# Last layer's mixer: gate projections in half blocks with two weight areas, a third convolution lane, gate columns taken together

## The reference

```
def _state_features(h, w_in_l, conv_l, a_log_l, dt_bias_l):
    p = h @ w_in_l[:, :N_STATE]
    ...
    gkv = jax.nn.silu(_dwconv(p[..., 2 * RET_W:2 * RET_W + 2 * GDN_W], conv_l[:, GDN_W:])).astype(jnp.float32)
    gk = _l2norm(_split_heads(gkv[..., :GDN_W], H_GDN))
    ...
    log_a = -jnp.exp(a_log_l.astype(jnp.float32))[:, None, :, None] * jax.nn.softplus(
        gab[0] + dt_bias_l.astype(jnp.float32)[:, None, :, None])
    beta = jax.nn.sigmoid(gab[1])
def _query_features(h, w_in_l, conv_l):
    ...
    gq = jax.nn.silu(_dwconv(p[..., 2 * RET_W:2 * RET_W + GDN_W], conv_l[:, :GDN_W])).astype(jnp.float32)
    gq = _l2norm(_split_heads(gq, H_GDN)) * GDN_DK ** -0.5
    gz = p[..., 2 * RET_W + GDN_W:2 * RET_W + 2 * GDN_W]
    gates = jax.nn.sigmoid(p[..., 2 * RET_W + 2 * GDN_W:].astype(jnp.float32))
def _mixer_out(ret_o, gdn_o, rg, gz, gates, ret_gn_w_l, gdn_norm_w_l, w_ret_out_l, w_gdn_out_l, w_o_l):
    ret_y = _merge_heads(_group_norm(ret_o)) * ret_gn_w_l.astype(jnp.float32) * jax.nn.silu(rg.astype(jnp.float32))
    gdn_y = _merge_heads(_head_rms(gdn_o)) * gdn_norm_w_l.astype(jnp.float32) * jax.nn.silu(gz.astype(jnp.float32))
    merged = (gates[..., :D_MODEL] * (ret_y.astype(dt) @ w_ret_out_l)
              + gates[..., D_MODEL:] * (gdn_y.astype(dt) @ w_gdn_out_l))
    return merged.astype(dt) @ w_o_l
```

## Time and profile before

| | us |
|---|---|
| median of 3 runs | 3236.97 (3236.73 to 3237.56) |
| profiled execution, its own time | 3248.51 |
| its span in the trace | 3246.7 |

### The profile page before, as it was taken

How to read it: one execution, slowest core, us unless ns; L and a number is a source line. 1 busy time by engine, 2 the same in 40 slices (tenths; PEclk the granted TensorE clock), 3 DMA queues, 4 the chain that set the end, 5 groups by cost and what they waited for, 6 DMA issues and landing times.

```text
span 3246.7 us, 29030 instructions
## 1 busy us (share of the span) xinstructions
PE 2499.2 (77%) x9500; PEld 1318.0 (41%) x9500; DVE 1623.4 (50%) x3307; ACT 835.9 (26%) x2259; POOL 831.3 (26%) x717
## 2 busy tenths in 40 slices
PE   6788897877979877888877777778787767576673
PEld 3665343423545455733322222456554433222221
DVE  4535645769876663565667654355524332111112
ACT  1212334243433230233343433223110101011110
POOL 1002332344546110133444433011010012222221
PEclk9689998998989977999999999888988779788886
DMA  6027997897979812499999999410112189999992
GB/s 254 1 78 288 368 366 293 324 396 272 371 296 371 338 52 78 168 405 414 416 421 395 421 422 421 164 65 26 52 52 109 76 338 397 393 386 384 383 375 84
DMA packets 128898, 885.92 MB, mean 273 GB/s; under 512 B 23008, under 2 KB 23392, under 8 KB 31584
## 3 DMA queue, kind: packets, MB, share of 16 engines
q0 software_dynamic: 86976, 553.74, 43.3%
q1 hardware_dynamic: 41760, 330.22, 25.4%
HBM read 877.56 MB, written 37.75 MB: 282 GB/s over the span
## 4 chain that ended last, share of the span: by engine, by line
PE 44%; DMA 24%; DVE 20%; ACT 5%; issue 4%; POOL 2%; SPq 1%; DVEq 0%; POOLq 0%; ACTq 0%
PE ps L155 43%; DMA ring<-in_peer_uv,idx_u 10%; DMA ring<-in_w_gu 5%; DVE ring L1256 5%; DVE arena L76 4%; ACT arena L125 3%; DMA ring<-in_w_down 3%; DMA arena<-in_w_gu 2%; DVE arena L97 1%; PE ps L158 1%; DVE ring L76 1%; DVE iu L113 1%; SPq L2479 1%; DVE arena L1256 1%; DMA ring<-in_w_in 1%
## 5 line engine op out<-in xcount | busy, mean ns | idle before, releaser
L155 PE MATMUL ps<-ring,arena 128*128 128x512 f32 (+3 forms) x3200 | 1239.6, 649 | 305.4 <-ACT arena L125 183.6
L155 PEld LDWEIGHTS ps<-ring,arena 128*128 128x128 f32 (+2 forms) x3200 | 459.5, 180 | 984.4 <-issue 593.9
L1256 DVE CUSTOM_DVE_ANT_0 ring<-ring,h 128x1024 f32<-128x1024 f32 x428 | 539.6, 1261 | 392.0 <-DMA ring<-in_peer_uv,idx_u 365.1
L155 PE MATMUL ps<-arena 128*128 128x128 f32 (+7 forms) x2184 | 514.4, 425 | 201.4 <-ACT arena L125 83.6
L2297 POOL DMA_INDIRECT ring<-in_peer_uv,idx_u x428 | 464.5, 1085 | 798.5 <-PE ps L155 667.0
L125 ACT ACTIVATE arena<-arena 128x1 f32<-128x1 f32 (+4 forms) x1121 | 309.6, 276 | 818.0 <-DVE arena L1256 731.9
L155 PEld LDWEIGHTS ps<-arena 128*128 128x128 f32 (+3 forms) x2184 | 296.6, 202 | 382.2 <-issue 153.9
L155 PE MATMUL ps<-ring,hT 128*128 128x512 f32 (+1 forms) x704 | 327.1, 621 | 44.2 <-DMA ring<-in_w_in 22.1
L76 DVE TENSOR_TENSOR arena<-arena,ps 128x512 f32<-128x512 f32 (+1 forms) x134 | 77.2, 576 | 449.0 <-ACT arena L125 353.3
L125 ACT ACTIVATE arena<-ps 128x512 f32<-128x512 f32 (+5 forms) x164 | 89.7, 547 | 762.5 <-PE ps L155 692.3
L125 ACT ACTIVATE arena<-cst,arena 128x128 f32<-128x128 f32 x512 | 206.3, 403 | 199.3 <-PE ps L155 159.8
(11 more groups left out here) (116 smaller groups left out, 1621.7 us busy)
## 6 DMA issues: line engine op xcount, KB each, us to landing
ring<-in_w_gu SPq DMA_DIRECT2D x98, 1024.0 KB, 30.3
ring<-in_w_down SPq DMA_DIRECT2D x52, 1024.0 KB, 22.6
ring<-in_w_in SPq DMA_DIRECT2D x22, 2048.0 KB, 9.1
arena<-in_w_gu SPq DMA_DIRECT2D x30, 1024.0 KB
ring<-in_w_mod SPq DMA_DIRECT2D x12, 2048.0 KB, 11.1
ring<-in_peer_wq SPq DMA_DIRECT2D x8, 2048.0 KB, 7.8
ring<-in_w_o SPq DMA_DIRECT2D x6, 2048.0 KB, 11.6
arena<-in_w_down SPq DMA_DIRECT2D x12, 1024.0 KB
```

What stands on the lines that cost most here:

```text
L155: return self.e.matmul(o, lhsT, rhs, start=start, stop=stop, skip_group_check=True)
L1256: v.done(v.e.tensor_tensor_reduce(out=row, in0=row, in1=h[:, n // 128, :], scale=1.0, scalar=0.0, op0=ALU.mult, op1=ALU.add, accum_out=aa[ ...
```

## The change

It does seven things.

1. The gate products come in 12 half blocks of 256 columns for both chunks, with half-size weights (`w_gates`), which lie in turn in areas 13 and 15. Half block j is computed in one piece in phase GATE_AT[j], as the last thing of that phase. ScalarE and VectorE take it in the next phase.
2. Gq gets a generator of its own, from phase 4 on, with scratch in the places of Oret and Ogdn. The fill of these with zeros goes from ahead of the feature stage to behind it.
3. `gate_columns` does the ScalarE steps function by function for both chunks, one phase later, and VectorE's last step two phases later. In the context rows all engines get two more phases.
4. `out_norm` has one more yield, ahead of the wait for the power.
5. The two halves of the w_o product change places.
6. The ACT and DVE lists put `gate_columns` at other places.
7. The weight table is cut on the host to fit.

```
+GATE_AT = (0, 1, 2, 3, 6, 9, 12, 15, 20, 21, 22, 26)
+GATE_PHASES = 30
...
+    def conv_scratch(self, lane):
+
+        if lane == 2:
+            return self.Oret.rearrange("p c n -> p (c n)"), self.Ogdn.rearrange("p c n -> p (c n)"), self.T(5)
+        return self.T(8 * lane, 2), self.T(8 * lane + 2, 2), self.T(8 * lane + 4)
...
-                      [("Rk", 0, 0), ("Rv", 1, 12), ("Rq", 4, 16)], [(0, "Gk", 4, 4), (2, "Gq", 0, 0)],
-                      [(1, "Gv", 8, 8)])
+                      [("Rk", 0, 0), ("Rv", 1, 12), ("Rq", 4, 16)], [(0, "Gk", 4, 4)], [(1, "Gv", 8, 8)],
+                      [(2, "Gq", 0, 0)])
...
             def gate_columns(s, xT, among, *ready):
                 yield from rows_mm((s.tag, "gab"), xT, gab_sb, 16, ("loaded", s.tag, "gab"), *ready,
                                    wstride=16, among=among)
+                yield from idle(2)
...
-                    conv_features(s, hT, s.conv_blocks2, 8, (4, 5), *ready), gate_columns(s, hT, (6, 7), *ready), idle(4))
+                    conv_features(s, hT, s.conv_blocks2, 1, (4, 5), *ready), gate_columns(s, hT, (6, 7), *ready),
+                    chain(idle(4), conv_features(s, hT, s.conv_blocks3, 2, (6, 7), *ready)), idle(4))
...
                 def gates():
-                    for i in range(6):
-                        for c in range(2):
-                            yield
-                            b = fresh("gate", i, c, among=(7,))
-                            pe.wait_ge(*at("loaded", "gate", i))
-                            for k in range(8):
-                                t = pe.mm(b[:, :], hT[:, k, c * P:(c + 1) * P], R(13, 4)[:, k * 512:(k + 1) * 512],
-                                          k == 0, k == 7)
-                                if k in (2, 5):
-                                    yield
-                            pe.done(t, ("ps", "gate", i, c))
-                        pe.tell(("used", "gate", i))
+                    for p in range(GATE_PHASES):
+                        for j in gates_at(p):
+                            b = fresh("gate", j, among=(7,))
+                            pe.wait_ge(*at("loaded", "gate", j))
+                            for c in range(2):
+                                for k in range(8):
+                                    t = pe.mm(b[:, c * 256:(c + 1) * 256], hT[:, k, c * P:(c + 1) * P],
+                                              gate_place(j)[:, k * 256:(k + 1) * 256], k == 0, k == 7)
+                            pe.done(t, ("ps", "gate", j), ("used", "gate", j))
+                        yield
...
-                for i, area in ((0, 7), (1, 0)):
+                for i, area in ((1, 0), (0, 7)):
                     run(rows_mm(("mo", i), hT, R(area, 4), 512, ("loaded", "w_o2", i), *ready))
...
             def second():
                 s = x_side
-                v.fill(ar(10240, 2048), 0.0)
...
-                    gate_columns(s), ret_matrix(s.T(15), s.T(14)[:, 0:P], s.T(14)[:, P:2 * P]))
+                run(row_features(s), conv_features(s, s.conv_blocks, 0), conv_features(s, s.conv_blocks2, 1),
+                    chain(idle(4), conv_features(s, s.conv_blocks3, 2)), ret_matrix(s.T(15), s.T(14)[:, 0:P], s.T(14)[:, P:2 * P]),
+                    gate_columns(s))
+                v.fill(ar(10240, 2048), 0.0)
...
                 def gates():
-                    for i in range(6):
-                        for c in range(2):
-                            for _ in range(3):
-                                yield
-                            if i < 2:
-                                x = (rg, gz)[i][:, c, :]
-                                v.wait_ge(*at("gate sigmoid", i, c))
-                                v.tt(x, x, tile_of("gate", i, c)[:, :], ALU.mult, ("out", "gate", i, c))
+                    for p in range(GATE_PHASES):
+                        yield
+                        for j in gates_at(p):
+                            if j < 4:
+                                x = (rg, gz)[j // 2][:, :, 256 * (j % 2):256 * (j % 2) + 256]
+                                v.wait_ge(*at("gate sigmoid", j))
+                                v.tt(x, x, tile_of("gate", j)[:, :].rearrange("p (c n) -> p c n", c=2), ALU.mult,
+                                     ("out", "gate", j))
...
                     v.tt(g[:, c, :], g[:, c, :], nw[:, o:o + 512], ALU.mult)
+                    yield
                     v.wait_ge(*at("y rstd", kind, c))
...
             def gate_columns(s):
-                for _ in range(3):
-                    yield
-                for c in range(2):
-                    e1, e2 = sc8["e1"], sc8["e2"]
+                yield from idle(4)
+                for c in range(2):
                     a.wait_ge(*at("out", s.tag, "gab", c))
                     a.act(be[:, c, :], be[:, c, :], ACT.Sigmoid, (s.tag, "beta", c))
-                    a.act(e2, e1, ACT.Abs)
-                    a.act(e2, e2, ACT.Exp, scale=-1.0)
-                    a.act(e2, e2, ACT.Ln, (s.tag, "softplus", c), bias=1.0)
+                    a.act(sc8[f"e2{c}"], sc8[f"e1{c}"], ACT.Abs)
+                for c in range(2):
+                    a.act(sc8[f"e2{c}"], sc8[f"e2{c}"], ACT.Exp, scale=-1.0)
+                for c in range(2):
+                    a.act(sc8[f"e2{c}"], sc8[f"e2{c}"], ACT.Ln, (s.tag, "softplus", c), bias=1.0)
+                yield
...
-            for i, b in enumerate((5, 7, 8, 9, 10, 11)):
-                block(13, 4, d["w_in2"][b], ("loaded", "gate", i),
-                      after=[("used", "gate", i - 1)] if i else [("used", "x", "Rv"), ("used", "x", "Rq")])
-            block(13, 4, d["w_gdn_out"], ("loaded", "merge", 1), after=[("used", "gate", 5)])
+            for j in range(12):
+                block(13 + 2 * (j % 2), 2, d["w_gates"][j], ("loaded", "gate", j),
+                      after=[("used", "gate", j - 2)] if j > 1 else [("used", "x", "Rv"), ("used", "x", "Rq")])
+            block(13, 4, d["w_gdn_out"], ("loaded", "merge", 1), after=[("used", "gate", 10), ("used", "gate", 11)])
```

73 lines of the change are left out of this document (40 added, 33 removed).

## The result

The changed kernel takes 3187.28 us (median of 4 runs, 3183.5 to 3189.15), the kernel before 3237.26 on the same chip (4 runs, 3236.73 to 3237.93): a ratio of 0.9844, 95% interval 0.9827 to 0.9861, 50 us less. The profiled execution of after took 3189.15 with a span of 3187.2, so it lies 0.06% above its median, where that of before lay 0.36% above.

The account below looks back on a forecast made before the run. TensorE was taken to set the mixer loop's pace, busy 215 of 266 us. Terms -28 - 4.8 - 3 - 6.6 - 4 + 5 = -41.4 gave 3195 us; own range 3188 to 3204, 8 in 10 3182 to 3208.

Parts of the forecast that it names:

- loop: Mixer loop, first product to the lanes' last: from 261.8 us to 234, 28 us less.
- feature stage with the fill's place: Last layer's feature stage: loop's first product 4.8 us earlier, 1.1 of it from the fill's place; bounds 1 and 7.
- output norms and w_o: Output norms 3 us less by powers under way early; w_o product 6.6 us less by weights that arrive in time.
- layer 0: gate columns, tail: Beside the gathers: three fewer table loads, 4 us less; context steps behind the last gather, net 5 more, bounds 0 and 9.
- half clock: TensorE at 1.2 GHz in the loop: 4 us at the start, 3.2 after the boundary, 2.7 after each of two U waits.
- the largest wait: Second chunk's start in the loop: TensorE waits about 8 and then 3.9 us for VectorE, 1.9 before it, 13.7 in all.
- more is won: Rival: full clock after U waits (5), context's tail free (5), half of VectorE's boundary chain hides; 3183, chance 0.13.
- nothing waits: Gate weights in the loop: the closest load has 12.6 us and needs 7.9, so waits 0; other bound 10 us.
- A second step: Layer 0: with the context's last steps out of the gather loop, the last gathers are issued about 3 us earlier.
- Chains that bound the loop: Rival: hand-overs between engines cost 0.1 to 0.3 us more, about 70 times; loop wins 14, 3209, chance 0.17.
- a drop to 1.2 GHz from the boundary on: Rival: TensorE stays at half clock from the second chunk's start, up to 76 us more, 3271; slower had chance 0.03.
- Late weights: Rival: gate half blocks 2, 3 and 10 each wait in the loop, 10 us and some clock; 3206, chance 0.05.

Follow-up runs that it names:

- u_gates: Changed kernel with the gates as before: whole blocks of 512 columns, three products per phase, one area of four places; 3222.6 us, ratio to before 0.9952.
- u_wo: Changed kernel with the w_o product's halves in the old order and no yield ahead of the output norms' power wait; 3193.6 us, ratio to before 0.9859.
- o_area: Changed kernel with all 12 gate half blocks in one area of two places, each load after the half block before; 3208.3 us, ratio to before 0.9908.
- u_gq: Changed kernel with Gq computed behind Gk in one generator again, as before; 3185.4 us, ratio to before 0.9835.
- c_loads: Changed kernel with ScalarE's gate column steps chunk by chunk again (7 table loads beside the gathers, 8 in the last layer); 3195.7 us, ratio to before 0.9868.
- t_steps: Changed kernel with three more background steps beside layer 0's gathers, so none is left behind the last gather; 3194.5 us, ratio to before 0.9857.
- g_two: Changed kernel with gate half blocks 8 and 9 in phases 18 and 19 instead of 20 and 21; 3187.3 us, ratio to before 0.9837.

## Why the prediction was right or wrong, point by point

| term | predicted | measured |
|---|---|---|
| loop | -28 | -36.4 (traces), -33 to -37 alone (u_gates) |
| feature stage with the fill's place | -4.8 | -2.3 to -3.2 |
| output norms and w_o | -9.6 | -8.6 (u_wo), -10.4 to -11.4 (traces) |
| layer 0: gate columns, tail | -4 and +5 | -14 at gathers 64 to 80; +5.6 from gather 80 to the last, +6.3 from its issue to the norm; net -5 by traces (3 of them ahead of gather 64), near 0 by medians |
| sum | -41.4 | -50 |

**The loop: right in its parts but one.** Predicted were 194 us of work, 28.5 of waits and 12.6 of half clock. The trace has 25.6 of waits (the rows above less the 3.2 ahead of the loop). Half clock is 2.4 us over the first groups (8 records in 2.07 us), and 2.5 behind the boundary (1.0 at AT, 1.45 at the half block of 8.52), 4.9 in all. That leaves 194.9 of work. (The three terms of the prediction add up to 235.1; I wrote 234, and those 1.1 us had no source.) The place of the largest wait was foreseen: 7.72 and 3.32 at AT where I had "about 8 and then 3.9". Of the 9.7 us between 235.1 and 225.4, the half clock is 7.7 and the waits 2.9, less 0.9 more work. The mis-sized term is the half clock: I had charged 5.4 us behind the waits at U, but there 24 records after a wait of 2.06 us took 2.94 (2.84 without a wait), full clock, and the start lost 2.4 instead of 4. This is the "more is won" rival in part; I had read the 2.41 us wait of the earlier trace rows as what a 2 us wait would do.

**Weights.** The bound I took, nothing waits, held. The figure of 7.9 us for a 1 MB load was too high: the ten loads in this loop landed in 4.9 us (median of the trace's issues). The formula in the Trainium skill, page "DMA: Bandwidth & Descriptors", section "Anatomy of one DMA", gave an estimate of 4.4, and that is nearer than my row of a 2 MB load. The section fits its formula to transfers that GpSimd issues, and these are issued by SyncE, so the agreement is this case's alone. In o_area, where it matters, this is the difference between 14 and over 20 us.

**The feature stage: the sum was half right and the reasons wrong.** Two steps failed. I let the wait of 4.99 us for ScalarE's sigmoid go because Gq's products stand there. It goes also without them: u_gq has none. In before the two sigmoids ahead of it waited 0.66 and 1.80 us for VectorE's convolutions, which stood behind its two stops for the logarithms; in u_gq they wait for nothing. And I walked VectorE's end to 2186.4 from about 2156, 30.4 us. From the same place it took 32.6 (2145.4 to 2178.0 in after), for it waited in it for GpSimd and for transposes (0.6 to 1.3 us each, six times, 6.6 in all), with hardly anything of another chain to fill them. The lane itself cost 4.5 us, a sign that I never gave it. Of the edit list only the rearranged gate columns paid in this stage (the fill's place took back 1.8 and gave 1.1).

**Output norms and w_o.** Right. Both waits went as walked: 3.0 us in four pieces and 5.6 us; the half clock in the product was 1.4 us (29.14 in the earlier trace rows, 27.70 now), within the 1.0 to 1.6.

**Layer 0.** Only the three table loads were priced. c_loads has them at about 4 us for gathers 64 to 80, against 3.84 by their durations. The Trainium skill, page "ScalarE: Activation LUTs", section "What ACT_TABLE_LOAD costs", with its drain of 1.38 us each would have made it 8; the runs side with the durations alone. What I missed stood in the same place: VectorE without a dot product for 11 us, which I had named ("VectorE no longer waits in the middle") and costed at nothing. The tail came out as walked, 12 operations and 8.3 us more behind the last dot product (12.7 against 4.4). That taking it away would win 5 us was wrong: t_steps does and wins nothing. A second step failed that I had at 3 us less: the stretch from gather 80 to the last took 533.4 and 535.6 us in the two traces of before and 536.3 to 544.5 in the nine of the changed order, so 5.6 more by the means, and no run says why. That layer 0 as a whole ended within 1 to 6 us of my +1 is therefore luck: the gain was 10 us too small, and the losses against it 7. By the medians it is near zero: 50 less the 36.4, 2.3 to 3.2 and 10.4 to 11.4 of the later stages leaves -1 to 1. By the norm's position in the traces (1097.5 as the mean of two before, 1092.5 of nine with the changed order) it is 5, and the two don't agree better than the scatter allows. This stays open.

**The rivals.** Chains that bound the loop and a drop to 1.2 GHz from the boundary on did not occur: the granted clock of the loop is 0.96, and TensorE's waits from the boundary's first P on are some 6 us. Late weights did not either. "More is won" had the right side: of its three reasons one holds (full clock behind the waits at U), one doesn't (the boundary's chain hides nowhere), and of the third, the tail, t_steps shows only that moving it among the gathers wins nothing.

## What to carry to other kernels

Cover is a matter of place, not only of amount: the same gate products, without any late weights, were worth 15 us more as whole pieces at the points where a chain runs through other engines, and moving them again was worth 1 or 6 us depending on whether each link of the chain was met. Price a moved or regrouped step by what the engines that wait for it could have done meanwhile; the few small operations of a neighbour stopped VectorE for 11 us and went with some 10 us of the gathers' time, three times the loads that one sees on the engine. Where an engine bounds the end of a stage, look for where that same engine idles earlier: a lane of its own that puts another engine's work ahead of what the bounding engine waits for can lengthen the stage.

## What the runs showed of the hardware

The half clock behind a wait isn't a matter of the wait's length alone. Behind 2.06 us at U, 24 records took 2.94 us in after. In g_two the same group behind a wait of 2.01 took 4.27:

```profile
2389.36 4.27 PE L155 MATMUL ps<-arena 128*128 128x128 f32 x24 [2.01 <-DVE arena L76]
```

Behind waits of 2.40 and 2.49 us the next groups ran at half clock in whole or in part (8 records in 2.08 us, a half block in 8.83), and behind 2.24 at full clock in o_area. What else decides it the runs don't tell. And a run of gathers moves the whole program by several us: with the same order up to the last gather, its issue came between 1066 and 1076 us in nine traces, while the last layer's stages repeated within about 1 us.
